# Per-head RMS norm of the HGRN2 read-out: sums spread by a matrix of ones, root and reciprocal over 512 columns

## The reference, cut to what matters

```
def hgrn_readout(o, p_g, onorm_g):
    y = o * lax.rsqrt(jnp.mean(o * o, axis=-1, keepdims=True) + EPS) * onorm_g.astype(jnp.float32)
    y = y.reshape(B, L, HGRN_WIDTH) * jax.nn.silu(p_g.astype(jnp.float32))
    return y.astype(p_g.dtype)
```

## Time and profile before

| | us |
|---|---|
| time, median of 3 runs (lowest to highest) | 1431.02 (1429.6 to 1432.42) |
| profiled execution, its own time | 1437.04 |
| profiled execution, span | 1435.2 |
| PE busy | 1373.4 (96%) |
| DVE busy | 770.9 (54%) |
| ACT busy | 382.3 (27%) |
| POOL busy | 317.5 (22%) |

### The profile page before, as it was taken

How to read it: one execution, slowest core, us unless ns; L and a number is a source line. 1 busy time by engine, 2 the same in 40 slices (tenths; PEclk the granted TensorE clock), 3 DMA queues, 4 the chain that set the end, 5 groups by cost and what they waited for, 6 DMA issues and landing times. The chain is left out here.

```text
span 1435.2 us, 17676 instructions
## 1 busy us (share of the span) xinstructions
PE 1373.4 (96%) x6805; PEld 1150.1 (80%) x6805; DVE 770.9 (54%) x976; ACT 382.3 (27%) x576; POOL 317.5 (22%) x137
## 2 busy tenths in 40 slices
PE   6899999999999988899989999999999999999998
PEld 2688888888888867687768888888888888888876
DVE  1798798888869799629622323223231313233227
ACT  3711322322222236426621111211111111211122
POOL 0521210111011151504532212212212122212110
PEclk8999999999999998999999999999999999999999
DMA  9361311230110020023321111211111111111132
GB/s 365 152 206 30 104 60 45 61 101 29 44 49 26 15 103 1 0 88 128 123 59 30 59 52 37 59 45 44 58 29 58 58 44 44 58 42 46 58 124 112
DMA packets 94715, 102.08 MB, mean 71 GB/s; under 512 B 3118, under 2 KB 77091, under 8 KB 94658
## 3 DMA queue, kind: packets, MB, share of 16 engines
q1 hardware_dynamic: 94658, 101.32, 21.1%
HBM read 92.92 MB, written 8.39 MB: 71 GB/s over the span
## 5 line engine op out<-in xcount | busy, mean ns | idle before, releaser
L1302 POOL TENSOR_TENSOR slot<-slotraw,slot 128x1024 fp32r<-128x1024 f32 x66 | 160.3, 2444 | 522.4 <-ACT slot L1238 309.9
L598 PE MATMUL bank<-h2Ta,slot 128*128 128x512 f32 x1056 | 247.5, 394 | 5.2 <-POOL slot L1302 4.9
L598 PE MATMUL bank<-slot,mid 128*128 128x512 f32 x1056 | 242.9, 391 | 1.8 <-POOL slot L1302 1.8
L598 PEld LDWEIGHTS bank<-h2Ta,slot 128*128 128x128 f32 x1056 | 200.4, 190 | 47.8 <-POOL slot L1302 5.3
L598 PEld LDWEIGHTS bank<-slot,mid 128*128 128x128 f32 x1056 | 199.3, 189 | 43.9 <-POOL slot L1302 2.2
L598 PE MATMUL bank<-cathi,slot 128*128 128x512 f32 x704 | 220.2, 389 | 0.0
L1521 DVE SCALAR_TENSOR_TENSOR cat<-conv_u,taps,cat 128x784 f32<-128x784 f32 (+29 forms) x120 | 150.1, 1251 | 10.2 <-DVE cat L1521 4.9
L598 PEld LDWEIGHTS bank<-cathi,slot 128*128 128x128 f32 x704 | 132.1, 188 | 27.8 <-issue 0.3
L1805 DVE TENSOR_TENSOR mid<-bank,sgm 128x512 f32<-128x512 f32 x44 | 30.4, 691 | 224.3 <-ACT sgm L1253 224.3
L598 PE MATMUL bank<-hT,ringb 128*128 128x512 f32 (+1 forms) x672 | 148.9, 378 | 0.0
L1830 DVE TENSOR_TENSOR arena<-bank,arena 128x512 f32<-128x512 f32 x144 | 99.5, 691 | 90.0 <-PE bank L598 89.5
(11 more groups left out here) (180 smaller groups left out, 1520.4 us busy)
## 6 DMA issues: line engine op xcount, KB each, us to landing
mraw<-in_w_mod SPq DMA_DIRECT2D x48, 512.0 KB, 6.2
slotraw<-in_ffn_w_gate SPq DMA_DIRECT2D x22, 512.0 KB, 3.7
slotraw<-in_ffn_w_up SPq DMA_DIRECT2D x22, 512.0 KB, 3.7
slotraw<-in_ffn_w_down SPq DMA_DIRECT2D x22, 512.0 KB, 4.2
ringinb<-in_w_in SPq DMA_DIRECT2D x12, 512.0 KB, 3.7
xst<-in_x SPq DMA_DIRECT2D x8, 512.0 KB, 12.8
ringina<-in_w_in SPq DMA_DIRECT2D x8, 512.0 KB, 3.7
ringinc<-in_w_in SPq DMA_DIRECT2D x8, 512.0 KB, 4.2
```

The costliest lines, as they stand in the source:

```text
L598: return pe.matmul(o, l, r, start=start, stop=stop, skip_group_check=True)
L1302: return pool.tensor_tensor(lo, full, hi.bitcast(F32), ALU.subtract)
```

## The change

The 8 "ssq" matmuls and the 8 "rb" matmuls of a head go. In their place stand two uses "ms", one for each half: one fp32 matmul with the 128x128 matrix of ones as the stationary operand and the 512 squares as the moving one, so that every partition of the bank holds the sums of 512 tokens. ACT takes the root from that bank over 512 columns, back into AT, and DVE takes the reciprocal in place over 512 columns, twice, where the one over 8 columns was. In unit 14 DVE multiplies cat by AT, from SBUF, and PE has nothing of the norm in that unit any more. A new semaphore, head_done, counts these multiplies, and ACT waits for it before it writes AT again at level 0 of the next head and before it splits finished tiles of cat. The hss tile is no longer used.

```diff
-USES += [("o", 0, 0), ("o", 1, 0), ("ssq", 0, 0), ("rb", 0, 0), ("rb", 1, 0)]
+USES += [("o", 0, 0), ("o", 1, 0), ("ms", 0, 0), ("ms", 1, 0)]
-USE_BY = ["act" if u[0] in ("turn", "ssq") or u[:2] == ("level", 0) else "dve" for u in USES]
+USE_BY = ["act" if u[0] in ("turn", "ms") or u[:2] == ("level", 0) else "dve" for u in USES]
-           "ssq": OUT_AT + 1, "rb": OUT_AT + 2}[_u[0]]
+           "ms": OUT_AT + 1}[_u[0]]
...
-                elif kind == "ssq":
-                    pe.wait_ge(sq_ready, h * 2 + 2)
-                    for ch in range(XT):
-                        ins = mm(b[:, ch:ch + 1], AT[:, ch * P:(ch + 1) * P], ones[:, 0:1], True, True)
                 else:
-                    if a1 == 0:
-                        pe.wait_ge(rs_ready, h + 1)
-                    for cc in range(4):
-                        ins = mm(b[:, cc * P:(cc + 1) * P], view(hss, XT + a1 * 4 + cc, [(0, P)]), ident[:],
-                                 True, True)
+                    pe.wait_ge(sq_ready, h * 2 + (a1 + 1))
+                    ins = mm(b[:], ones[:], AT[:, a1 * BANK:(a1 + 1) * BANK], True, True)
...
                     act.wait_ge(use_full, h * NUSE + (i + 1))
+                    act.wait_ge(head_done, h * 2 + 2)
                     act.activation(AT[:, a2 * BANK:(a2 + 1) * BANK], b[:], ACT.Copy).then_inc(use_act, 1)
...
-                elif kind == "ssq":
+                elif kind == "ms":
                     act.wait_ge(use_full, h * NUSE + (i + 1))
-                    act.activation(hss[:, 0, :], b[:, 0:XT], ACT.Sqrt, bias=eps[:], scale=1.0 / P).then_inc(use_act, 1)
+                    act.activation(AT[:, a1 * BANK:(a1 + 1) * BANK], b[:], ACT.Sqrt, bias=eps[:],
+                                   scale=1.0 / P).then_inc(use_act, 1)
...
-            act.wait_ge(use_dve, HEADS * N_UDVE)
+            act.wait_ge(head_done, 2 * HEADS)
...
-                act.wait_ge(use_dve, (HEADS + 1) * N_UDVE - 1 + hf)
+                act.wait_ge(head_done, 2 * HEADS + 1 + hf)
...
                 elif u == OUT_AT + 1:
-                    dve.wait_ge(use_act, h * N_UACT + 2 * N_UACT)
-                    dve.reciprocal(hss[:, 1, :], hss[:, 0, :]).then_inc(rs_ready, 1)
+                    for hf in range(2):
+                        a = AT[:, hf * BANK:(hf + 1) * BANK]
+                        dve.wait_ge(use_act, h * N_UACT + (2 * N_UACT - 1 + hf))
+                        dve.reciprocal(a, a).then_inc(rs_ready, 1)
                 elif u == OUT_AT + 2:
                     for hf in range(2):
-                        i = USES.index(("rb", hf, 0))
-                        dve.wait_ge(use_full, h * NUSE + (i + 1))
-                        dve.wait_ge(use_dve, h * N_UDVE + (2 * N_UDVE - 3 + hf))
-                        c = cat_tile(h)[:, hf * BANK:(hf + 1) * BANK]
-                        dve.tensor_tensor(c, bank[LBASE + i % LRING][:], c, ALU.mult).then_inc(use_dve, 1)
+                        sl = slice(hf * BANK, (hf + 1) * BANK)
+                        dve.wait_ge(rs_ready, h * 2 + (hf + 1))
+                        dve.wait_ge(use_dve, h * N_UDVE + (2 * N_UDVE - 1 + hf))
+                        dve.tensor_tensor(cat_tile(h)[:, sl], AT[:, sl], cat_tile(h)[:, sl],
+                                          ALU.mult).then_inc(head_done, 1)
```

More of the change, by code:

```diff
@@ L330, in kernel_program @@
         state_done, sq_ready, rs_ready, conv_done = sem("state_done"), sem("sq_ready"), sem("rs_ready"), sem("conv_done")
+        head_done = sem("head_done")
         tail_full, tail_act, tail_dve = sem("tail_full"), sem("tail_act"), sem("tail_dve")
@@ L1374, in _ @@
             dve.sem_inc(use_dve, N_UDVE)
+            dve.sem_inc(head_done, 2)
             dve.sem_inc(down_free, 4)
```

## The result

The changed kernel took 1459.74 us (median of 4, 1458.67 to 1460.89) against 1431.72 for the kernel before: a ratio of 1.0178, 95% interval 1.0162 to 1.0194, slower by 25 us by that ratio and by 28 by the medians. Measured again beside later runs it took 1457.80, ratio 1.0148 (1.0133 to 1.0164); there the kernel before read 1436.04. So the loss is 21 to 28 us, and experiments are compared by their ratios. The lower figure is the better founded one: it rests on 22 executions of the kernel before (1431.47 to 1437.91), the higher one on four that all lie at the low end of that range (1429.6 to 1433.65).

What follows compares the result with a forecast made beforehand. PE was taken to wait once per head, after the norm, for DVE: 6.2 + 6.2 + 6.0 (gates) + 4.0 (clock) + 4.2 (last head) = 26.6 us on 1431.0, so 1457.6 us, range 1447 to 1467.

Steps and rivals of the forecast that it cites:

- The bound: Once per head, just after the norm, PE waits at a gate DVE opens; PE's savings ahead of it are waited away.
- The reciprocal: On DVE, 512 columns take 3.2 us each, from the 1- and 8-column rows; DVE is 6.2 us later per head.
- eight cycles a column: Reading of the skill's reciprocal rule: 8.3 ns a column, some 4.4 us for 512 columns, whole sum about +36 us.
- The rivals with a steep and with an ordinary slope: Reciprocal of 512 columns: 4.1 us, giving 1465, chance 0.18; or 0.69 us, +2.6 in all, chance 0.04.
- The gates: PE's waits for DVE after heads 0, 1 and 2: later by 6.2, 6.2 and 6.0 us.
- The 3.33 us at the loop's jump: DVE's idle time before the keys in pass 2, taken as the jump's price, which doesn't shrink.
- DVE then works without a gap: From the tail's start at 512.58 to the Q that PE awaits at 537.30; part of that gate's +6.0.
- The clock: PE's clock lowered after the longer waits before unit 1 of passes 2 and 3: 2.0 us twice, +4.
- The last head: Head 3, without cover: roots, reciprocals and multiplies delay mix(0) by 4.2 us.
- That slack takes part of it: Rival: DVE's lateness fills the 3.33 us before the keys in pass 2, clock not lowered; 1450, chance 0.20.
- That PE sets the pace: Rival: DVE's additions disappear in its idle time and PE keeps 1.7 us per head; 1424, chance 0.03.

Runs made afterwards that it cites:

- 16 memsets: 16 memsets of an unused tile at the start of DVE's program, against the changed kernel with the inverse root on ACT and no DVE reciprocals; 1437.93 us, ratio 1.0015.

## Why the prediction was right, step by step

The forecast was 1457.6 us, 26.6 more than the median shown; measured were 1459.74 and 28.0 more, by the second occasion 1457.80 and 21.8 more. The direction, the gates and the size of the reciprocal were right. The sum was some 5 us too high against the better measure of the loss and against the traces (21.7), and most of that is one term, the clock.

- **The bound.** Right: the share of 54% hid that DVE opens a gate for PE after every norm. The run with PE's work tripled shows that PE's time there is waited away but for a few microseconds, the run with the reciprocals added to the kernel before shows that DVE's counts.
- **The reciprocal.** 3.2 us from the slope between 1 and 8 columns; 3.32 measured, a slope of (3320 - 154)/511 = 6.2 ns per column where I had 6.0. The reading of the Trainium skill (VectorE: DVE Perf Modes, Walkthrough: the 8-slice pipeline in each mode) as eight cycles a column would have given 4.4 by estimate; the measurement decides against that reading. The rivals with a steep and with an ordinary slope fall with it.
- **The gates.** 6.2, 6.2 and 6.0 against 7.5, 5.9 and 6.6. PE's waits there add up to 8.8, 5.0 and 12.5 us; I had 8 to 9 for each pass, too much for pass 3, where nothing was waited before, and about 9 for the tail. The first is over because of where the 2 us delays fall. The changed kernel has two of them in its taps (5.52 us for three, 6.57 for four), the kernel before has none there, with 4.67 for four, but one later:

```profile
261.04 3.64 DVE L1521 SCALAR_TENSOR_TENSOR cat<-conv_u,taps,cat 128x880 f32 x3
...
277.34 3.73 DVE L1541 TENSOR_SCALAR F<-F 128x2560 f32<-128x2560 f32 x1
```

  The changed kernel takes 1.49 for that last one, so it has one delay more. The 3.33 us at the loop's jump stayed, 3.37, and the row now names no releaser, which bears out that it isn't a wait; that it is a fixed price of the jump was too strong, since 16 memsets brought it to 0.85. "DVE then works without a gap" in the tail left out what DVE worked on: some 13 of the 24 us up to Q are such delays, six of them, as in these rows of the kernel before, where like instructions take 1.48 us and, for two, 1.29. Taken off, they leave nothing of PE's wait of 6.26 us.

```profile
522.12 3.65 DVE L1545 TENSOR_TENSOR T<-F 128x1280 f32<-128x1280 f32 x1
...
531.57 5.58 DVE L1576 TENSOR_TENSOR Q<-Q,F 128x512 f32<-128x512 f32 x2
```

- **The clock.** +4 us, and this step failed: 0 arrived at the two gates that it was for. I put the long waits before unit 1, whose matmuls PE does on its own account. In fact they come before level 0, and the slow matmuls are level 0's, with the wait for the row behind them. The windows of the changed kernel show it (us, PE, PEld, DVE, ACT, POOL, PEclk):

```profile
284.00:291.00 7.00, 5.81 (x32) 5.62 (x32) 6.93 (x7) 1.15 (x3) 0.00 (x0) 0.66 0.00 1
291.00:296.00 5.00, 4.22 (x18) 3.49 (x19) 2.80 (x4) 1.46 (x2) 0.00 (x0) 1.00 0.36 105
```

  Full clock is back for unit 1. Where a wait of 3.35 us did fall in front of unit 1, in the run with short reciprocals, that unit took 8.28 us for 5.73, so the price was real and its place wrong:

```profile
278.79 3.84 PE L599 MATMUL bank<-qraw,K 128*128 128x128 f32 x32 [1.40 <-DVE K L1532]
285.98 8.28 PE L599 MATMUL bank<-hT,ringa 128*128 128x512 f32 x24 [3.35 <-DVE mod L1428]
```

  In the tail, where I put the clock at nothing new, a part did arrive. Level 0 runs slowly after its wait (6.59 us, in the kernel before 3.84), and DVE then waits 1.58 us for level 1 behind it:

```profile
555.14 1.29 DVE L1573 TENSOR_TENSOR Q<-Q,F 128x512 f32<-128x512 f32 x2 [1.58 <-PE bank L599]
```

- **The last head.** +4.2 against 4.3, from the sums to mix(0); two reciprocals and two roots account for it, the root taking 0.68 where I had the square's 0.60.
- **A slip.** The matmuls at 537.30 in the earlier trace rows are level 2's, not level 1's; level 1 stands at 528.22 in the earlier trace rows. The chain and its price are the same. In the changed kernel most of that wait has moved to level 0.
- **The rivals.** That slack takes part of it fell: the 3.37 us are still there. That PE sets the pace fell with the tripled matmuls.

Against the two traces the sum comes out so: 26.6, less 4.0 for the clock, 1.6 more for the gates, 0.6 in the tail before the sums and 0.1 for the last head give 24.9. The 0.8 and the 2.5 us outside the change take it to 21.6, the measured 21.7. So the nearness of 26.6 to the 28.0 of the first occasion is luck in part: the four executions of the kernel before that it is reckoned from were low ones, and that hides the clock term.

## What to carry to other kernels

Ask at which wait an engine's time is cashed in before pricing a saving: an engine busy for 96% can be waiting, once per loop passage, for one that is busy for 54%, and then the latter's work counts nearly one to one and its own hardly at all. Spreading a sum over all partitions makes every later step pay for 128 copies of it; where that step is a reciprocal on DVE, 8 columns at 0.2 us become 1024 at 6.6. And a small result that another engine waits for belongs ahead of long work in its producer's order: that edit alone brought 0.3%. And price a lowered clock at the work that follows the wait, asking whether that work is itself waited for: 7.39 us of wait ahead of level 0 cost nothing through the clock, 3.35 us ahead of unit 1 cost 1.5 to 2.9.

## What the runs showed of the hardware

The reciprocal runs at 6.2 ns per column, an ordinary multiply of 512 columns at 0.68 us in all. ACT has an inverse root, Abs_reciprocal_sqrt, that takes the place of root and reciprocal in one pass; with it one more table load of 1.28 us stands at the next root, and the kernel has 18 loads for 16. Some twenty single DVE instructions in a trace are about 2 us longer than their like (3.56 against 1.49 for the same L1540). Which they are is the same in both traces of the changed kernel; the place of the code decides it for some, and a longer program of PE, with DVE's unchanged, shifts some too. That this is the loading of the program is possible and not shown. The Trainium skill (Runtime: NRT & Kernel Launch, Instruction fetch mechanics) says that a taken branch forces a fetch of the target before execution goes on, when the target lies outside the part of the program that the engine holds. The gap at DVE's jump, 0.85 to 5.46 us by placement alone or with small edits, would fit that; no run here shows what it is made of. After a wait PE's granted clock can fall to half (1.2 GHz): the windows of the changed kernel have 0.66 over level 0 after 7.39 us, and after 3.35 us in front of unit 1 its 24 matmuls took up to 8.58 us for 5.73.
